# A two-block transformer kernel: retention rotations read from PSUM, the cT transposes and copy, the gate Sigmoids and some weight loads moved

## The reference

```python
h = rmsnorm(x, norm_mix[layer])
(q, kc, vc, ks, vs, kw, vw, nsa_g, rq, rk, rv, rg, gate_a, gate_b) = jnp.split(h @ w_in[layer], offsets, axis=-1)
# compressed keys and values: windows of 32 tokens through a small MLP
blk = k[cmp_idx] + pe[None, :, None, :]
k_cmp, v_cmp = silu(blk @ w1) @ w2
p_c = softmax(where(valid, q . k_cmp * scale, NEG));  o_c = p_c @ v_cmp
o = gi[..., 0:1] * o_c + gi[..., 1:2] * o_s + gi[..., 2:3] * o_w      # gi = sigmoid(nsa_g)
# retention: rotary on rq and rk, halves x1, x2 of each head
out = concatenate([x1 * cos - x2 * sin, x1 * sin + x2 * cos])
```

## Time and profile before

| what | us |
|---|---|
| median of 3 executions | 990.83 |
| lowest and highest | 990.08, 992.43 |
| the profiled execution | 992.43 |
| its span, first to last instruction | 990.4 |
| TensorE, VectorE, ScalarE busy | 964.9, 631.8, 507.6 |

### The profile page before, as it was taken

One profiled execution on the slowest core, in us unless ns is written; L12 is line 12 of the kernel. 1 busy time (PEld: TensorE's weight loads), 2 busy tenths in 40 slices (PEclk: granted clock), 3 DMA queues, 4 the chain that ended last, 5 costly groups with the idle time before them and its releaser, 6 DMA issues.

```text
span 990.4 us, 15893 instructions
## 1 busy us (share of the span) xinstructions
PE 964.9 (97%) x6552; PEld 872.5 (88%) x6552; DVE 631.8 (64%) x822; ACT 507.6 (51%) x746; POOL 52.3 (5%) x88
## 2 busy tenths in 40 slices
PE   7999999999999999999999999999999999999996
PEld 5877889989999888988988899998998899999995
DVE  5667576676655555778867687775654556555544
ACT  5565655555544444556545475544555354444442
POOL 4000000002000000300000002100200020000000
PEclk9999999999999999999999999999999999999999
DMA  8974344554665556455554446564745356565651
GB/s 288 328 249 128 94 126 101 171 192 147 215 194 188 184 179 197 121 187 179 166 156 127 131 140 199 156 197 138 228 155 170 120 158 197 179 197 176 196 183 43
DMA packets 134935, 170.36 MB, mean 172 GB/s; under 512 B 7648, under 2 KB 99088, under 8 KB 134864
## 3 DMA queue, kind: packets, MB, share of 16 engines
q1 hardware_dynamic: 133472, 165.47, 54.3%
q10 hardware_dynamic: 848, 2.58, 0.8%
q0 software_dynamic: 544, 1.31, 0.4%
...
## 4 chain that ended last, share of the span: by engine, by line
PE 83%; DVE 8%; ACT 4%; issue 3%; DMA 1%; POOL 0%; SPq 0%; ACTq 0%; DVEq 0%; POOLq 0%
PE ps L356 13%; PE ps L357 13%; PE ps L358 13%; PE ps L386 6%; PE ps L387 5%; PE ps L388 5%; PE ps L693 5%; PE ps L692 5%; PE ps L694 5%; PE ps L339 4%; PE ps L435 3%; DVE room L1430 3%; DVE parts L1396 2%; ACT parts L950 2%; DVE room L1436 1%
## 5 line engine op out<-in xcount | busy, mean ns | idle before, releaser
L1396 DVE TENSOR_TENSOR parts<-raws,parts 128x1024 fp32r<-128x1024 f32 (+1 forms) x308 | 367.9, 1211 | 238.5 <-ACT parts L950 237.5
L950 ACT ACTIVATE parts<-raws 128x1024 fp32r<-128x1024 f32 (+1 forms) x308 | 315.3, 1043 | 252.0 <-PE ps L358 141.8
L356 PE MATMUL ps<-room_r,parts 128*128 128x256 f32 x1248 | 352.5, 282 | 3.0 <-DVE parts L1396 3.0
L358 PE MATMUL ps<-room_r,parts 128*128 128x256 f32 x1248 | 348.5, 279 | 0.0
L357 PE MATMUL ps<-room_r,parts 128*128 128x256 f32 x1248 | 348.4, 279 | 0.0
L356 PEld LDWEIGHTS ps<-room_r,parts 128*128 128x128 f32 x1248 | 234.6, 188 | 9.0 <-issue 3.9
L357 PEld LDWEIGHTS ps<-room_r,parts 128*128 128x128 f32 x1248 | 234.7, 188 | 1.4
L358 PEld LDWEIGHTS ps<-room_r,parts 128*128 128x128 f32 x1248 | 234.6, 188 | 0.0
L386 PE MATMUL ps<-parts,room_r 128*128 128x512 f32 (+1 forms) x336 | 136.2, 405 | 3.0 <-DVE parts L1396 3.0
L387 PE MATMUL ps<-parts,room_r 128*128 128x512 f32 (+1 forms) x336 | 131.6, 392 | 0.0
L388 PE MATMUL ps<-parts,room_r 128*128 128x512 f32 (+1 forms) x336 | 131.5, 391 | 0.0
...
## 6 DMA issues: line engine op xcount, KB each, us to landing
...
```

Source lines behind the costliest of these rows:

```text
L356: e.matmul(ps, wh, hT[0][:, k, :], start=k == 0, stop=False)
L358: last = e.matmul(ps, wl, hT[0][:, k, :], start=False, stop=k == K - 1)
L950: e.activation(t.h, t.raw, ACT.Copy).then_inc(s["hi"], 1)
L1396: e.tensor_tensor(t.l, t.raw, t.h.bitcast(F32), ALU.subtract).then_inc(s["lo"], 1)
```

## The change

It does these things:

- the retention rotations read `rq` and `rk` straight from PSUM and free the bank themselves, with sine and cosine that four new VectorE pieces have scaled by rstd (`r_sin`, `r_cos`, in `junk`); ScalarE's copies of `rq` and `rk` are gone, and the rotations are due at the group's end and no longer four counts later
- the Sigmoids of `gsig` stand right behind the copies of `qkv` and no longer behind the window copies; VectorE's `coef` pieces move forward with them, and tile 16's rest comes before the NSA rotations
- TensorE does `cmp_T` behind `scores` 0 and 1, two transposes and two steps, and VectorE and no longer ScalarE copies cT to `pcT`
- ScalarE's `scores(p)` has no `until(... + 3)` any more
- two `until` bounds in the SSD stage are gone
- the w1 quarters go behind tiles 6, 8, 10, 12, 14, 16, 18 and 20 (they were behind 6, 8, 10, 11, 16, 17, 18 and 20).

```diff
--- before.py
+++ after.py
@@ -167,6 +167,7 @@
         tmp = [tmp_all[:, 512 * i:512 * i + 512] for i in range(4)]
         qkv = r1.take(2 * 1560).rearrange("p (t n) -> p t n", t=2)
         sin, cos = (r1.take(144).rearrange("p (t f) -> p t f", t=2) for _ in range(2))
+        r_sin, r_cos = (junk[:, i:i + 128].rearrange("p (t f) -> p t f", t=2) for i in (0, 128))
         half_of = lambda g: slice(64 * g, 64 * g + 64)
@@ -636,12 +637,12 @@
                     last = group(psum[:, b, h * P:h * P + P], pairs)
                 ends(last, ("RO", t), b)
-            cmp_T()
             for p in range(2):
                 scores(p)
             turn_r("rqT", rq, 0)
             turn_r("rkT", rk, 0)
             step(2)
+            cmp_T()
             probs_T(0)
             for p in range(8):
                 t = p // 4
@@ -1076,6 +1077,11 @@
                 e.activation(tab, red[:, 0:144].rearrange("p (t f) -> p t f", t=2), ACT.Sin).then_inc(s["trig"], 1)
             qkv_out(1)
             qkv_out(2)
+            for t in range(2):
+                out_of(("qkv", 2, t))
+                e.activation(gsig[:, t, :, :], qkv[:, t, 64 * NG:64 * NG + 24].rearrange("p (h b) -> p h b", b=3),
+                             ACT.Sigmoid).then_inc(s["gsig"], 1)
+
             def tm_out(dst, name, blocks, u, f=ACT.Copy):
                 for blk in range(blocks):
                     for t in range(2):
@@ -1086,8 +1092,6 @@
                                      scale=scaled(u, t)).then_inc(taken[g.bank], 1)
             def projections():
-                yield from tm_out(rq, "rq", 1, MIX)
-                yield from tm_out(rk, "rk", 1, MIX)
                 yield from tm_out(rv, "rv", 1, MIX)
                 yield from tm_out(rg, "rg", 1, MIX, ACT.Silu)
@@ -1101,10 +1105,6 @@
                 step(e.activation(A[0:64, :, :], T[0:64, :, 0::2], ACT.Copy))
                 step(e.activation(A[64:P, 0, :], T[64:P, 1, 1::2], ACT.Copy))
                 emptied(e.activation(A[64:P, 1, :], T[64:P, 0, 1::2], ACT.Copy), ("win", i))
-            for t in range(2):
-                out_of(("qkv", 2, t))
-                e.activation(gsig[:, t, :, :], qkv[:, t, 64 * NG:64 * NG + 24].rearrange("p (h b) -> p h b", b=3),
-                             ACT.Sigmoid).then_inc(s["gsig"], 1)
             for i in range(2):
                 copy_out(hid_rows[i], psum[:, where["hid", i].bank, 0:256], ("hid", i))
             copy_out(hid[0], psum[:, where["hidT", 0].bank, 0:60].rearrange("p (c n) -> p c n", c=2), ("hidT", 0), ACT.Silu)
@@ -1133,7 +1133,6 @@
             def scores(p):
                 nk = P * (p // 4 + 1)
                 full(("S", p, 1))
-                until(where["S", p, 1].at + 3)
                 if p >= 2:
                     e.wait_ge(s["pe"], where["PT", p - 2, (p - 2) // 4].at)
                 e.wait_ge(s["nmax"], p + 1)
@@ -1155,7 +1154,6 @@
                 for n in range(p // 4 + 1):
                     copy_out(pT[:, 512 * n:512 * n + 512], psum[:, where["PT", p, n].bank, :], ("PT", p, n))
-            copy_out(pcT[0:120, :], psum[0:120, where["cT"].bank, 0:256], "cT")
             for p in range(2):
                 scores(p)
             turned(rqT, "rqT", 0)
@@ -1232,7 +1230,6 @@
             e.wait_ge(s["pad"], 1)
             conv_in(0)
             conv_in(1)
-            until(where["cv", 2].at + 2)
             for t in range(2):
                 e.wait_ge(s["zrstd"], t + 1)
                 e.activation(x[:, t, :], z[:, t, :], ACT.Copy, scale=rstd[sq_of[MIX2]][t]).then_inc(s["y"], 1)
@@ -1562,7 +1559,7 @@
             rotated = {"q_rot": 0, "r_rot": 0}
-            def rotate(o1, o2, i1, i2, c, sn, shape, sem):
+            def rotate(o1, o2, i1, i2, c, sn, shape, sem, name=None):
                 n = int(np.prod(shape[1:]))
                 names = " ".join("abc"[:len(shape) - 1])
@@ -1573,12 +1570,17 @@
                 step(tt(v[0], i1, c, ALU.mult))
                 step(tt(v[1], i2, sn, ALU.mult))
                 step(tt(v[2], i1, sn, ALU.mult))
-                step(tt(v[3], i2, c, ALU.mult))
-                settle()
+                if name is None:
+                    step(tt(v[3], i2, c, ALU.mult))
+                    settle()
+                else:
+                    emptied(tt(v[3], i2, c, ALU.mult), name)
+                    settle()
+                    out_of(name)
                 tt(o1, v[0], v[1], ALU.subtract).then_inc(s[sem], 1)
                 tt(o2, v[2], v[3], ALU.add).then_inc(s[sem], 1)
-            until(where["qkv", 2, 1].at)
+            until(where["qkv", 2, 1].at + 1)
             e.wait_ge(s["trig"], 2)
             for t in range(2):
                 for blk in range(3):
@@ -1589,22 +1591,33 @@
                        [P, 2, nh, 8], "q_rot")
             e.wait_ge(s["q_rot"], 6)
             e.tensor_copy(heads[:, :, KC + 2:VC + 3:3, :], heads[:, :, KC:VC + 1:3, :]).then_inc(s["again"], 1)
+            e.wait_ge(s["rstd"], 2)
+            for t in range(2):
+                for to, tab in ((r_sin, sin), (r_cos, cos)):
+                    step(ts(to[:, t, :], tab[:, t, 8:72], rstd[sq_of[MIX]][t], ALU.mult))
+            settle()
             spread(MIX)
             def rotations():
                 for name, dst in (("rq", rq), ("rk", rk)):
                     for t in range(2):
-                        yield where[name, 0, t].at + 4
-                        out_of((name, 0, t))
+                        g = where[name, 0, t]
+                        yield g.at
+                        e.wait_ge(s["pe"], g.at)
+                        v = psum[:, g.bank, :].rearrange("p (h s d) -> p h s d", h=4, s=2)
                         o = dst[:, t, :].rearrange("p (h s d) -> p h s d", h=4, s=2)
-                        rotate(o[:, :, 0, :], o[:, :, 1, :], o[:, :, 0, :], o[:, :, 1, :],
-                               bc(cos[:, t, 8:72], 1, [P, 4, 64]), bc(sin[:, t, 8:72], 1, [P, 4, 64]),
-                               [P, 4, 64], "r_rot")
+                        rotate(o[:, :, 0, :], o[:, :, 1, :], v[:, :, 0, :], v[:, :, 1, :],
+                               bc(r_cos[:, t, :], 1, [P, 4, 64]), bc(r_sin[:, t, :], 1, [P, 4, 64]),
+                               [P, 4, 64], "r_rot", (name, 0, t))
                 yield from fm_out(sig1, "sig", 8)
                 yield from gated(0, sig1)
             put_behind(rotations())
+
+            e.wait_ge(s["gsig"], 2)
+            for t in range(2):
+                step(ts(coef[:, t, :, 1:2], gsig[:, t, :, 0:1], const("crow")[:, t:t + 1], ALU.mult))
             for i, pe_col in enumerate(("pe_k", "pe_v")):
                 until(where["win", i].at)
                 out_of(("win", i))
@@ -1612,12 +1625,8 @@
                 src = bass.AP(A.tensor, A.offset, [list(A.ap[0]), [1, 16], [128, 2], [8, 15]])
                 tt(win_b[i][:, 0:480].rearrange("p (j g c) -> p j g c", j=16, g=2), src,
                    col(pe_col).unsqueeze(2).unsqueeze(3).to_broadcast([P, 16, 2, 15]), ALU.add).then_inc(s["windows"], 1)
-            until(where["vc"].at)
-
-            e.wait_ge(s["gsig"], 2)
-            for t in range(2):
-                step(ts(coef[:, t, :, 1:2], gsig[:, t, :, 0:1], const("crow")[:, t:t + 1], ALU.mult))
             full("vc")
+            e.wait_ge(s["consts"], 16)
             e.wait_ge(s["r_rot"], 8)
             emptied(tt(vc[0:120, :].rearrange("p (h d) -> p h d", d=64), bc(bank_of("vc")[0:120, 0:64], 1, [120, 8, 64]),
                        bc(const("own")[0:120, :], 2, [120, 8, 64]), ALU.mult), "vc")
@@ -1680,6 +1689,8 @@
             scores(0)
             scores(1)
             weigh(0)
+            full("cT")
+            emptied(e.tensor_copy(pcT[0:120, :], bank_of("cT")[0:120, 0:256]), "cT")
             for p in range(8):
                 if p in (5, 7):
                     t = (p - 5) // 2
@@ -2126,16 +2136,14 @@
             xin = a["x"].rearrange("b (t p) d -> p (b t) d", p=P)
             e.dma_start(ident, a["ident"]).then_inc(s["ident"], 16)
             e.dma_start(x[:, 1, :], xin[:, 1, :]).then_inc(s["x1"], 16)
-
-            w1_behind = {6: 0, 8: 1, 10: 2, 11: 3, 16: 4, 17: 5, 18: 6, 20: 7}
             for t in tiles:
                 if t.i >= RAW:
                     before = tiles[t.i - RAW]
                     e.wait_ge(s["lo"], before.i + 1)
                 for to, v in t.srcs:
                     e.dma_start(to, v).then_inc(landed[t.slot], 16)
-                n = w1_behind.get(t.i)
-                if n is not None:
+                n = (t.i - 6) // 2
+                if t.i % 2 == 0 and 0 <= n < 8:
                     name, to, w1 = ("w1k", w1k, a["cmp_k_w1"][0]) if n < 4 else ("w1v", w1v, a["cmp_v_w1"][0])
                     j = 4 * (n % 4)
                     e.dma_start(to[:, j:j + 4, :], w1[j * P:(j + 4) * P, :].rearrange("(k p) n -> p k n", p=P)).then_inc(s[name], 16)
```

## The result

| | before | after |
|---|---|---|
| median, us | 991.63 (4 executions) | 1000.89 (4 executions) |
| lowest and highest | 990.08, 992.62 | 999.40, 1002.15 |
| the profiled execution, its span | 992.43, 990.4 | 1002.52, 1000.6 |
| its mean granted clock | 0.997 | 0.989 |

The changed kernel takes 1.0094 times as long, with a 95% interval of 1.0074 to 1.0115: it is slower by 9.3 us, where 5.0 were forecast, and the time lies above the range. In the page of after, part 1 (the row that answers to the earlier trace rows) has TensorE busy for 4.9 us longer, with the same 6552 matmuls, and the other engines within 3 us of before.

The account below looks back on a forecast made before the run. TensorE, busy 97% of the span, was taken as the bound, so new waits add time: 4.9 - 2.0 - 1.1 + 3.0 - 0.9 + 1.1 = +5.0 us on the median 990.83, forecast 996.0, range 992 to 999.5.

Parts of the forecast that it names:

- Part 1: SyncE's queue: the moved w1 loads make tile 15 land at 46.6, 2.9 us later, bounds 0 and 2.9.
- part 2: ScalarE and VectorE before the NSA rotations: tile 16 starts at 50.1, not 45.63, and the rotations at 52.35, not 45.89.
- Part 3: VectorE's way to window 0: both `rq` rotations stand ahead of it, `hidden` 0 starts at 67.65, not 62.76, +4.9 us.
- the forecast's bound of +2.0 without part 1: The price at `hidden` 0, +2.0 us instead of +4.9, if the moved w1 loads cost nothing.
- Part 4: cT behind two steps: -2.0 us of wait at the second `scores`, -1.1 of half clock, +3.0 new wait at `scores` 2.
- the net -0.1: At `scores` 2, what moving cT was to change in all: -2.0, -1.1 and +3.0 us.
- part 5: Attention loop, Exp before the tile roundings: -0.9 us at `scores` 3, later roundings priced at 0; `scores` 2 at about 106.6.
- I put 0 on it, at most 2: Attention loop: rounding pairs coming up to 2 us later cost 0, at most 2 us once their cover is gone.
- tiles come late in the attention loop: Rival for the attention loop: 2 us or more of late roundings turn into waits, 998 to 1000 us; chance 0.11.
- The -0.9 at `scores` 3: TensorE's 0.94 us wait for an Exp at `scores` 3 goes, worth -0.9 us.
- Part 6: Granted clock behind the new TensorE waits: one stretch at the lower clock, +1.1 us, bounds 0 and 2.2.
- a shift that grows after 126: Sign against the forecast, which had all starts from 126 us on shifted by one constant.

Follow-up runs that it names:

- a_start: The changed kernel with the cT part and the order of Exp and roundings both put back as before: 994.05 us, ratio 1.0026 to the kernel before.
- a_w1: The changed kernel with the w1 loads back at their old places in SyncE's queue: 999.11 us, ratio 1.0077 to the kernel before.
- b_rot: The kernel before with only the rotations of `rq` and `rk` straight from PSUM: 992.21 us, ratio 1.0000 to the kernel before.
- a_ct: The changed kernel with cT's transposes ahead of `scores` 0 again and ScalarE copying them out: 996.57 us, ratio 1.0047 to the kernel before.
- a_rot: The changed kernel with the rotations as before, from ScalarE's copies of `rq` and `rk`: 998.02 us, ratio 1.0052 to the kernel before.
- a_sig: The changed kernel with the Sigmoids behind the window copies again and `coef` behind vc: 999.43 us, ratio 1.0082 to the kernel before.
- b_conv: The kernel before with only the two bounds ahead of the third convolution pair dropped: 991.38 us, ratio 0.9994 to the kernel before.
- a_ct_first: The changed kernel with VectorE copying cT out ahead of the rests of tiles 30 and 31: 1000.85 us, ratio 1.0083 to the kernel before.

## Why the prediction was right in direction and too small

**Part 1** was right on tile 15 to 0.5 us (46.6 forecast, 47.10 after and 46.58 alone), **part 2** to 0.4 on tile 16 (50.1 and 50.48) and on the start of the rotations (52.35 and 52.70). Behind the table load of 1.28 us at 48.95 the Sigmoid starts at 50.24. The Trainium skill (ScalarE: Activation LUTs, What ACT_TABLE_LOAD costs) adds a drain of 1.38 us; no row here shows it.

**Part 3** forecast `hidden` 0 at 67.65, it came at 68.23. The rotation from PSUM was priced like the one from SBUF, 2.13, and its pitch is 2.38 (61.20 to 63.58), with gaps of 0.11 us ahead of the last two pieces and 0.10 behind them, where the code waits for the bank and for the pieces before. The order of VectorE was read rightly. But the price belongs to the three parts together, as the alone runs show, and as a part of the time they cost 2.6 us and not 4.9 (`a_start`), since the rotations give something back at `scores` 1; the forecast's bound of +2.0 without part 1 fits `a_w1` (64.74 is +2.0).

**Part 4.** The trace meets the net -0.1: `scores` 2 is shifted as much as `scores` 0. The wait was 3.54 and not 3.0 (ScalarE starts the two roundings at 103.48, so tile 31 near 104.4 and not 103.7). The old half clock was worth more than the 1.1 counted from two groups: it lasts to 96.3, and from the wait ahead of `scores` 1 to the matmul that starts at 96.25 before and 97.72 after the shift falls by 3.8, 1.97 of wait and 1.8 of clock. The place of `scores` 2 in part 5, "about 106.6", doesn't follow from the terms, which give 107.0; it came at 107.44. Yet the step was wrong as a price. It counted -3.1 for leaving the wait at `scores` 1, and most of that would have gone anyway, with the rotations of part 3 (0.72 left of 1.97, no half clock: `b_rot`, `a_ct`). Against that the part cost 3.54 and, by the clock at 107.9, about 1.5. Undone it gives back 4.3 us, and alone it costs 0.38%, 3.8 us.

**Part 5 is the step that failed.** "I put 0 on it, at most 2": it is 2.40 us at `scores` 6 and 1.5 of half clock behind it, 4.0 of the 5.1 us that the sum lacks; alone 0.37%, 3.7 us. The two sentences under the 0 were both true, five `parts` buffers and ten microseconds between two tile pairs: no wait of TensorE for a tile appeared. What was left out is what stands behind the rests on VectorE. A rest that waits for a late rounding holds up all of VectorE, and the retention products and the `nsaT` rest, which empty the PSUM banks that `scores` 6 wants, are in that queue. The rival "tiles come late in the attention loop" (998 to 1000, chance 0.11) came nearest: it had the late roundings, but as waits for tiles, and it lacked the clock. The 1.5 us of clock are not certain either: `a_ct`, `a_rot` and `a_sig` have the wait (2.12 to 2.40 us) without it. The -0.9 at `scores` 3 was right (no wait there).

**Part 6** counted one stretch of 1.1 us. Four stand in the trace from 63 to 450 us: the one at 63.6 cost little, under the wait for window 0 (0.55 left), those at 107.9, 148.9 and 449.3 about 1.5 each; 0.8 of the last come back at 455.12, where before has a wait of 0.58. The conv bounds are worth 0, as forecast (`b_conv`).

Set against the runs, in us: parts 1 to 3 were put at 4.9 and cost 2.6 (`a_start`); part 4, with the 1.1 of part 6, at 1.0 and costs 3.8 alone; part 5 at -0.9 and costs 3.7 alone. The three add up to 10.1, of the same size as the 9.3 of the whole.

The sign that was to show the forecast wrong, "a shift that grows after 126", is what the trace has: +5.78 at 126, +9.80 at 159.

**Not settled**: `a_ct_first`, where a wait 3.4 us shorter left the median as it was; and what each of parts 1 to 3 adds to the time, which the intervals don't separate.
